# Weight low parts of the second block subtracted on VectorE

## The chip, the cores and the metric

The kernel runs on one core of a Trainium2 chip. The metric is the device time of one execution in microseconds (us). A core has TensorE (PE, matmuls; its weight loads are shown as PEld), VectorE (DVE), ScalarE (ACT), GpSimd (POOL) and SyncE (SP), which here issues the loads of weights. The engines run on their own and meet only at semaphores. Each engine works off its instructions in the order in which they were written, so a wait holds up all that stands behind it on that engine.

## What is computed

Two transformer-like blocks over 512 tokens of width 1024, in float32. The first has a half-step FFN, a mixer of two attentions, and another FFN. The second block, which the change is about, has two layers of this form (cut to what matters):

```python
def hybrid_mixer(h, ...):
    proj = h @ w_in
    qkv, z_a, a_lg, b_lg, cf_val, cf_glu, z_b, gate_lg = split(proj)
    qkv = silu(depthwise_conv_centred(qkv, qkv_conv_w))        # 5 taps, 12 tiles
    q, k, v = split(qkv); q = l2_normalize(q); k = l2_normalize(k)
    o = gated_delta(q, k, v, g_fwd) + flip(gated_delta(flip(q, k, v), g_bwd))
    o = rms(o) * dn_norm_w * silu(z_a)
    u = cf_val * sigmoid(cf_glu)
    u = depthwise_conv_centred(u, cf_conv_w) + cf_conv_b       # 31 taps, 4 tiles
    u = silu(layer_norm(u, cf_ln_w, cf_ln_b)) * silu(z_b)
    gate = sigmoid(gate_lg + gate_b)
    return (gate[0] * (o @ w_dn_out) + gate[1] * (u @ w_cf_out)) @ w_out
```

## The kernel before

**Weights as a stream.** All large weights come as 300 *units* of 128x1024 float32 (512 KB), in the order of use. 132 belong to the two FFNs, 48 to the mixer, 60 to each layer of the second block (the first of them is unit 180). Four slots (`RING`) hold them. Per unit: SyncE loads `raw` once the unit four before is used up; ScalarE casts it to `whi` (a rounded high part, L769); GpSimd subtracts, `wlo = raw - whi` (L1653), in place of `raw`; TensorE then makes three matmuls for each of the eight 128x128 tiles (L303 to L305: high by high, high by low, low by high), in `multiply`. TensorE waits on the semaphore `wlo` before a unit's first matmul. `AHEAD` is 2: cast and subtraction stand in the queues of their engines two units before the unit's use.

**A layer's stages.** `layer` in each engine's function goes through: eight units of value and glu gate (`up`); twelve projection units for q, k and v with the 5-tap convolution on VectorE (L1497 and four times L1500 per tile), the squares and the normalization (`unit_length`, L1485 and L1486); two lead gate units; the delta stage, which is a chunked triangular solve for two directions; eight units for the two `z`; two last gate units; and the merge with eight units of output and eight of the last projection.

**The delta stage** has four chunks (`i`). In each, both directions pass `decay`, `turn`, six levels (a matmul pair, `b.U` on VectorE in L1592, a matmul, `copy_predicated` in L1597; names `level1`, `join1` and so on), then `last`, `keys`, `values`, `out`, and the state update on VectorE (L1603, L1605 or L1607, L1610), on which the next chunk's first matmuls (`d_pre`, L674) wait through `d_snew`. A table, `DELTA_SLOTS`, puts twelve gate units tile by tile into TensorE's time at these named points; ScalarE and GpSimd have a `fill(i, point)` that issues the cast and the subtraction of the unit two ahead where the table starts a unit. Between the answers VectorE works off 56 taps of the 31-tap convolution (`conv(1)`, L1436); the fourth channel's taps are multiplied on ScalarE (L968) and added on GpSimd (L1680).

**The z stage**: VectorE multiplies by `z` (L1541) and splits off low parts (L1544) in a loop of eight.

Of the kernel before, what the change touches and what calls it, by code (L numbers as in the profile page):

```python
# [58 lines left out]
for _name, _n in (("norm", 8), ("qkv_w", 12 * QKV_TAPS), ("cf_w", 4 * CF_TAPS), ("cf_b", 4), ("ln_w", 4),  # L59
# [84 lines left out]
    "wlo xl_even xl_odd unit pair sums scale spread mid ml xr rope rot kc2 vxr vturn blk z1 cmp1 in_mix hidden "  # L144
    "cmp2 kc_raw kc_rot in_w1v kcc vtok vc_raw gate_row cmask expd score probs pt0 pt1 ptc turned o_new pv cw "
    "cturn vcc gts cscore ysum mix_lo h_new yl up wab_lo ab cp ab_raw ab_t sq_qkv ab_read decay sums_qkv l2 gl "
    "cum cum_s filled conv shared mean o_sq o_sums cu_sq var o_dn d_snew d_vns d_pre d_kk d_onew d_qk d_qd "
    "d_at d_a d_t d_u d_ys d_y d_att d_us d_uy d_ttk d_ttv d_kd d_kc d_vt d_kcs d_s0 d_vn d_s d_q d_o in_par "
    "raw0 raw1 raw2 raw3 whi in_h0 in_h1 in_h2 in_h3 square root y xh angle trig sil mh poly tanh gts_sig "
    "negmax csub cexp mix_hi sg yh prod glu_sig qconv qkv root_qkv zero soft_dve soft_act d_eg cum_d d_exp "  # L150
    "z_used cu_c o_root root_cu cu_n cu_silu d_neg d_min d_dec eps dve_step in_pos d_t0 h_out wab_hi out_dma "
# [143 lines left out]
def tensor_engine(pe, m, s):  # L295
# [235 lines left out]
    def merge(g):  # L531
# [4 lines left out]
        for c in range(KD):  # L536
# [3 lines left out]
            pe.wait_ge(s.wlo, u0 + c + 1)  # L540
# [1351 lines left out]
```

## Time and profile before

| | |
|---|---|
| median of three runs | 2611.58 us (2608.43 to 2611.78) |
| the profiled execution | 2605.9 us, of it span 2604.6 us |
| TensorE busy | 2396.9 us (92%) |
| VectorE busy | 1198.7 us (46%) |
| ScalarE busy | 920.5 us (35%) |
| GpSimd busy | 877.7 us (34%), of it L1653 736.9 us |
| chain that ended last | TensorE 76%, VectorE 16%, ScalarE 6%, GpSimd 0% |

Busy time says how long an engine had an instruction running, whether it moved or stood. The chain follows back from the last instruction what released each step. "Idle before" is the time in which an engine had nothing running before an instruction, with the releaser whose signal ended it. The granted clock is the share of full speed that TensorE was given.

### The profile page before, as it was taken

How to read it: one execution, taken by the hardware profiler on the slowest of the kernel's cores; microseconds unless marked ns; L12 is line 12 of the kernel's file. 1: busy time of each engine (PE TensorE's matmuls, PEld its weight loads, DVE VectorE, ACT ScalarE, POOL GpSimd, SP SyncE). 2: the span in 40 equal slices, each digit the busy share in tenths (PEclk: the TensorE clock that was granted, in tenths of full speed). 3: DMA queues.
4: the chain of work that ended last, by engine and by line, in shares of the span. 5: the costliest groups of instructions: out<-in, count | busy, mean ns of one | idle time of the engine just before them, and what ended most of it. 6: DMA issues, size and time to landing. Idle time of an engine off the chain costs nothing.

```text
span 2604.6 us, 29540 instructions
## 1 busy us (share of the span) xinstructions
PE 2396.9 (92%) x12132; PEld 1963.3 (75%) x12132; DVE 1198.7 (46%) x1825; ACT 920.5 (35%) x1532; POOL 877.7 (34%) x428
## 2 busy tenths in 40 slices
PE   5999998989999989999979779999998959999898
PEld 4888786776665868887867568997786748899686
DVE  3000124645655320001247976665536796666632
ACT  3222233233344432222333534444323534433432
POOL 3444443310111444444424522221344433222142
PEclk9999998989999989999979889999998989999998
DMA  3222222200011222222212100000222210000122
GB/s 149 97 98 97 97 97 90 81 25 25 25 33 41 90 69 97 96 96 95 97 41 89 57 25 25 25 25 33 81 98 71 77 47 17 25 26 25 46 96 77
DMA packets 46198, 169.41 MB, mean 65 GB/s; under 512 B 5232, under 2 KB 6000, under 8 KB 45808
## 3 DMA queue, kind: packets, MB, share of 16 engines
q1 hardware_dynamic: 45344, 165.73, 18.6%
q8 instruction: 97, 1.59, 0.2%
q10 hardware_dynamic: 720, 1.79, 0.2%
q14 instruction: 37, 0.30, 0.0%
HBM read 165.40 MB, written 2.10 MB: 64 GB/s over the span
## 4 chain that ended last, share of the span: by engine, by line
PE 76%; DVE 16%; ACT 6%; issue 2%; DMA 0%; POOL 0%; ACTq 0%; DVEq 0%
PE ps L303 18%; PE ps L305 18%; PE ps L304 18%; PE ps L694 4%; PE ps L702 3%; DVE acc L1500 3%; DVE ps L1485 2%; PE ps L691 2%; PE ps L483 2%; PE ps L449 2%; DVE rt L1200 1%; DVE ps L1526 1%; PE ps L464 1%; DVE acc L1497 1%; PE ps L320 1%
## 5 line engine op out<-in xcount | busy, mean ns | idle before, releaser
L1653 POOL TENSOR_TENSOR wlo<-raw,whi 128x1024 fp32r<-128x1024 f32 x300 | 736.9, 2457 | 1331.6 <-ACT whi L769 1331.6
L303 PE MATMUL ps<-xh,whi 128*128 128x512 f32 x1728 | 719.7, 417 | 88.9 <-DVE qkv L1486 28.4
L304 PE MATMUL ps<-xl,whi 128*128 128x512 f32 x1728 | 685.8, 397 | 0.0
L305 PE MATMUL ps<-xh,wlo 128*128 128x512 f32 x1728 | 685.3, 397 | 0.0
L303 PEld LDWEIGHTS ps<-xh,whi 128*128 128x128 f32 x1728 | 332.6, 192 | 197.2 <-issue 50.6
L769 ACT CAST whi<-raw 128x1024 fp32r<-128x1024 f32 x300 | 313.7, 1046 | 271.6 <-DMA raw<-in_stream 196.2
L305 PEld LDWEIGHTS ps<-xh,wlo 128*128 128x128 f32 x1728 | 331.7, 192 | 72.8
L304 PEld LDWEIGHTS ps<-xl,whi 128*128 128x128 f32 x1728 | 333.6, 193 | 64.2 <-issue 4.1
L1236 DVE TENSOR_TENSOR mid<-sil,ps 128x512 f32<-128x512 f32 x44 | 30.3, 688 | 442.8 <-PE ps L305 439.2
L1680 POOL TENSOR_TENSOR cu<-cu,prod 128x512 f32<-128x512 f32 x60 | 83.5, 1391 | 231.1 <-ACT prod L968 231.1
L1436 DVE SCALAR_TENSOR_TENSOR cu<-up,lcols,cu 128x512 f32<-128x512 f32 x180 | 160.0, 909 | 0.7
L303 PE MATMUL ps<-mh,whi 128*128 128x512 f32 x352 | 137.8, 392 | 4.1 <-DVE ml L1239 4.1
L305 PE MATMUL ps<-mh,wlo 128*128 128x512 f32 x352 | 137.6, 391 | 0.0
L304 PE MATMUL ps<-ml,whi 128*128 128x512 f32 x352 | 137.5, 391 | 0.0
L1239 DVE TENSOR_TENSOR ml<-mid,mh 128x512 fp32r<-128x512 f32 x44 | 50.9, 1160 | 175.4 <-ACT mh L812 175.4
L1115 ACT COPY dl<-ps 128x512 f32<-128x512 f32 x96 | 56.3, 586 | 199.7 <-PE ps L694 199.7
L805 ACT ACTIVATE sil<-ps 128x512 f32<-128x512 f32 x44 | 26.3, 598 | 274.7 <-PE ps L305 274.7
L1500 DVE SCALAR_TENSOR_TENSOR acc<-cp,lcols,acc 128x512 f32<-128x512 f32 x96 | 113.6, 1183 | 3.4
L694 PE MATMUL ps<-dl,rt 128*128 128x128 f32 x768 | 107.8, 286 | 0.0
L694 PEld LDWEIGHTS ps<-dl,rt 128*128 128x128 f32 x768 | 99.5, 202 | 0.0
L1597 DVE COPY_PREDICATED dl<-levels,ps 128x512 f32<-128x512 uint8 x96 | 70.5, 738 | 57.4 <-PE ps L702 57.1
L702 PEld LDWEIGHTS ps<-dl 128*128 128x128 f32 x768 | 93.1, 191 | 4.0
(288 smaller groups left out, 3393.6 us busy)
## 6 DMA issues: line engine op xcount, KB each, us to landing
raw<-in_stream SPq DMA_DIRECT2D x300, 512.0 KB, 3.2
w1k<-in_w SPq DMA_DIRECT2D x1, 2048.0 KB, 16.0
w1v<-in_w SPq DMA_DIRECT2D x1, 2048.0 KB, 8.0
outT<-h SPq DMA_DIRECT2D x4, 512.0 KB, 2.7
h<-in_xT ACTq DMA_DIRECT2D x2, 512.0 KB, 6.3
h<-in_xT SPq DMA_DIRECT2D x2, 512.0 KB, 5.9
mats<-in_mats ACTq DMA_DIRECT2D x1, 448.0 KB, 10.3
msk<-in_masks SPq DMA_DIRECT2D x1, 258.0 KB, 12.0
```

Of the source, the lines that this page charges most:

```text
L303: pe.matmul(out, wh, hi, start=first, stop=False)
L304: pe.matmul(out, wh, lo, start=False, stop=False)
L305: return pe.matmul(out, wl, hi, start=False, stop=last)
L694: heads(lambda n, hs: pe.matmul(X[0][:, hs], b.AT[:, n, :], b.T[:, n, :], start=True, stop=True)).then_inc(s.d_y)
L702: heads(lambda n, hs: pe.matmul(X[2][:, hs], b.U[:, n, :], b.Y[:, n, :], start=True, stop=True)).then_inc(s.d_uy)
L769: act.copy(m.whi[:, slot, :], m.raw[:, slot, :]).then_inc(s.whi)
L1115: act.copy(b.Y, X[0]).then_inc(s.d_ys)
L1436: ins = dve.scalar_tensor_tensor(out=dst, in0=src, scalar=w, in1=dst, op0=ALU.mult, op1=ALU.add)
L1500: ins = dve.scalar_tensor_tensor(out=acc, in0=cp[:, k:k + S], scalar=w, in1=acc, op0=ALU.mult, op1=ALU.add)
L1597: dve.copy_predicated(b.T, all_heads(m.levels[:, d, lv, :]), X[2]).then_inc(s.d_t)
L1653: pool.tensor_tensor(m.wlo[:, slot, :], m.raw[:, slot, :], m.whi[:, slot, :].bitcast(F32), ALU.subtract).then_inc(s.wlo)
L1680: pool.tensor_tensor(m.cu[:, 3, :], m.cu[:, 3, :], m.prod[:, k % 2, :], ALU.add).then_inc(s.shared)
```

## The change

The units from the third of the second block on (`POOL_UNITS` = 182 to 299, 118 units) get their low part from VectorE, with a semaphore of its own, `wlo_dve`; GpSimd keeps the first 182. TensorE waits for the one or the other (`low_part`). Everything else stays: the instruction's operands and size, the taps that GpSimd adds, the casts on ScalarE. The core of the diff:

```diff
+POOL_UNITS = 2 * U_FFN + U_MIX + AHEAD
...
+    def low_part(u):
+
+        if u < POOL_UNITS:
+            pe.wait_ge(s.wlo, u + 1)
+        else:
+            pe.wait_ge(s.wlo_dve, u - POOL_UNITS + 1)
...
+    split = POOL_UNITS
+
+    def weights_upto(u):
+
+        nonlocal split
+        while split < min(u, N_UNITS):
+            slot = split % RING
+            dve.wait_ge(s.whi, split + 1)
+            dve.tensor_tensor(m.wlo[:, slot, :], m.raw[:, slot, :], m.whi[:, slot, :].bitcast(F32),
+                              ALU.subtract).then_inc(s.wlo_dve)
+            split += 1
...
         for j in range(12):
             acc, cp = m.acc[:, j % 2, :], m.cp[:, j % 2, :]
+            weights_upto(u0 + L_QKV + j + AHEAD + 1)
             dve.wait_ge(s.cp, 12 * l + j + 1)
...
+        weights_upto(u0 + L_GATE + AHEAD + 1)
         for n in range(4):
             unit_length(4 + n, n)
...
+        weights_upto(u0 + L_GATE + LEAD_UNITS + AHEAD)
         dve.wait_ge(s.d_exp, l + 1)
         delta(l, cf_tap)
+        weights_upto(u0 + L_Z + AHEAD + 2)
...
         for n in range(8):
+            weights_upto(u0 + L_Z + n + AHEAD + 1)
             dve.wait_ge(s.filled, 24 * l + DELTA_UNITS + n + 1)
...
+        def fill(i, point):
+            for n, t0, t1 in DELTA_SLOTS[i, point]:
+                if t0 == 0:
+                    weights_upto(U0_LAYER[l] + L_GATE + n + AHEAD + 1)
...
+                if lv < nl:
+                    fill(i, f"level{lv}")
                 conv(1)
                 if lv < nl:
                     for d, at, X, b, t in both:
                         dve.wait_ge(s.d_uy, level_event(nl - 1, at, lv))
                         dve.copy_predicated(b.T, all_heads(m.levels[:, d, lv, :]), X[2]).then_inc(s.d_t)
+                    fill(i, f"join{lv}")
                     conv(1)
+            for point in ("last", "keys", "values", "out"):
+                fill(i, point)
             for d, at, X, b, t in both:
                 et = m.dsm[:, 3, t, 4 * d:4 * d + 4]
...
-        while split < min(u, N_UNITS):
+        while split < min(u, POOL_UNITS):
```

The same call stands before the tiles of the glu stage, at `decay` and `turn`, and in the merges. In the rows below, the changed kernel's own line numbers stand: L1198 is the new subtraction, and L1461, L1524, L1527, L1633, L1640, L1649, L1651, L1656, L1573 and L1576 are the old L1436, L1497, L1500, L1592, L1597, L1603, L1605, L1610, L1541 and L1544.

First, VectorE in the 5-tap convolution of the first layer. Before, two tiles:

```order
650 L1497 TENSOR_SCALAR acc<-cp,lcols 128x512
651 L1500 SCALAR_TENSOR_TENSOR acc<-cp,lcols,acc 128x512 x4
652 L1497 TENSOR_SCALAR acc<-cp,lcols 128x512
653 L1500 SCALAR_TENSOR_TENSOR acc<-cp,lcols,acc 128x512 x4
654 L1468 TENSOR_SCALAR small<-small 128x32
```

The same two tiles in the changed kernel:

```order
721 L1198 TENSOR_TENSOR wlo<-raw,whi 128x1024 [waits s_whi]
722 L1524 TENSOR_SCALAR acc<-cp,lcols 128x512 [waits s_qkv,s_cp]
723 L1527 SCALAR_TENSOR_TENSOR acc<-cp,lcols,acc 128x512 [waits s_dve_step] x4
724 L1198 TENSOR_TENSOR wlo<-raw,whi 128x1024 [waits s_whi]
725 L1524 TENSOR_SCALAR acc<-cp,lcols 128x512 [waits s_qkv,s_cp]
726 L1527 SCALAR_TENSOR_TENSOR acc<-cp,lcols,acc 128x512 [waits s_dve_step] x4
727 L1494 TENSOR_SCALAR small<-small 128x32 [waits s_soft_act]
```

One subtraction stands before each tile's five instructions.

Second, VectorE in the first chunk of the delta stage, in its third level (changed kernel):

```order
797 L1633 TENSOR_TENSOR dl<-ps,small 128x512 [waits s_d_u] x2
798 L1198 TENSOR_TENSOR wlo<-raw,whi 128x1024 [waits s_whi]
799 L1461 SCALAR_TENSOR_TENSOR cu<-up,lcols,cu 128x512 [waits s_dve_step]
800 L1640 COPY_PREDICATED dl<-levels,ps 128x512 [waits s_d_uy] x2
801 L1461 SCALAR_TENSOR_TENSOR cu<-up,lcols,cu 128x512 [waits s_dve_step]
```

and at that chunk's end, before

```order
727 L1592 TENSOR_TENSOR dl<-ps,small 128x512 x2
728 L1436 SCALAR_TENSOR_TENSOR cu<-up,lcols,cu 128x512
729 L1603 TENSOR_TENSOR rt<-rt,dsm 128x512
730 L1605 COPY o<-ps 128x4x128
731 L1610 TENSOR_TENSOR rt<-rt,ps 128x512
```

and now:

```order
814 L1633 TENSOR_TENSOR dl<-ps,small 128x512 [waits s_d_u] x2
815 L1461 SCALAR_TENSOR_TENSOR cu<-up,lcols,cu 128x512 [waits s_dve_step]
816 L1198 TENSOR_TENSOR wlo<-raw,whi 128x1024 [waits s_whi] x2
817 L1649 TENSOR_TENSOR rt<-rt,dsm 128x512 [waits s_d_o]
818 L1651 COPY o<-ps 128x4x128
819 L1656 TENSOR_TENSOR rt<-rt,ps 128x512 [waits s_dve_step,s_d_s]
```

The subtraction of unit 25 of the layer stands between `b.U` and the tap; those of units 26 and 27 stand between the last tap and the state update.

Third, VectorE in the z stage, in the changed kernel:

```order
905 L1573 TENSOR_TENSOR cu<-cu,prod 128x512
906 L1576 TENSOR_TENSOR fl<-cu,fh 128x512
907 L1573 TENSOR_TENSOR cu<-cu,prod 128x512
908 L1576 TENSOR_TENSOR fl<-cu,fh 128x512
909 L1198 TENSOR_TENSOR wlo<-raw,whi 128x1024
910 L1573 TENSOR_TENSOR cu<-cu,prod 128x512
911 L1576 TENSOR_TENSOR fl<-cu,fh 128x512
```

Row 909 is unit 38 of the layer; on GpSimd nothing stood ahead of it but the subtraction of unit 37.

## Rows read from the trace of the kernel before

**Rows 1.** The page: busy times, and the chain that ended last by engine.

```profile
PE 2396.9 (92%) x12132; PEld 1963.3 (75%) x12132; DVE 1198.7 (46%) x1825; ACT 920.5 (35%) x1532; POOL 877.7 (34%) x428
...
PE 76%; DVE 16%; ACT 6%; issue 2%; DMA 0%; POOL 0%; ACTq 0%; DVEq 0%
```

**Rows 2.** Groups by line and shape: busy us, mean ns, idle before, releaser.

```profile
L1653 POOL TENSOR_TENSOR wlo<-raw,whi 128x1024 fp32r<-128x1024 f32 x300 | 736.9, 2457 | 1331.6 <-ACT whi L769 1331.6
...
L1500 DVE SCALAR_TENSOR_TENSOR acc<-cp,lcols,acc 128x512 f32<-128x512 f32 x96 | 113.6, 1183 | 3.4
...
L1328 DVE TENSOR_REDUCE st<-ps 128x2 f32<-128x1024 f32 x8 | 9.8, 1224 | 0.3
```

**Rows 3.** Timeline of VectorE, convolution and unit_length: start us, us, what, idle.

```profile
1421.61 2.56 DVE L1497 TENSOR_SCALAR acc<-cp,lcols 128x512 f32<-128x512 f32 x1 [4.02 <-ACT cp L1011]
1424.20 6.12 DVE L1500 SCALAR_TENSOR_TENSOR acc<-cp,lcols,acc 128x512 f32<-128x512 f32 x4
...
1437.21 0.48 DVE L1497 TENSOR_SCALAR acc<-cp,lcols 128x512 f32<-128x512 f32 x1
1437.73 3.11 DVE L1500 SCALAR_TENSOR_TENSOR acc<-cp,lcols,acc 128x512 f32<-128x512 f32 x4
...
1486.30 3.36 DVE L1485 RECIPROCAL ps<-ps 128x512 f32<-128x512 f32 x1
...
1508.78 3.37 DVE L1485 RECIPROCAL ps<-ps 128x512 f32<-128x512 f32 x1 [2.86 <-ACT ps L1002]
```

**Rows 4.** Timeline of GpSimd in the same stretch.

```profile
1424.88 1.29 POOL L1680 TENSOR_TENSOR cu<-cu,prod 128x512 f32<-128x512 f32 x1 [1.00 <-ACT prod L968]
1426.13 2.86 POOL L1653 TENSOR_TENSOR wlo<-raw,whi 128x1024 fp32r<-128x1024 f32 x1
```

**Rows 5.** Stretches: length, busy us of PE, PEld, DVE, ACT, POOL; PEclk, DMA.

```profile
1480.00:1486.00 6.00, 0.00 (x0) 0.00 (x0) 5.86 (x5) 2.14 (x4) 4.34 (x3) 0.50 0.00 0
...
1836.00:1842.00 6.00, 5.34 (x17) 4.29 (x18) 4.48 (x5) 4.15 (x7) 2.88 (x2) 0.72 0.00 0
```

**Rows 6.** Timeline of all engines, first chunk of the delta stage, third level.

```profile
1556.34 0.74 DVE L1436 SCALAR_TENSOR_TENSOR cu<-up,lcols,cu 128x512 f32<-128x512 f32 x1
...
1557.10 1.05 ACT L769 CAST whi<-raw 128x1024 fp32r<-128x1024 f32 x1
...
1558.05 0.72 ACT L968 ACTIVATE prod<-up,lcols 128x512 f32<-128x512 f32 x1
1558.20 0.74 DVE L1597 COPY_PREDICATED dl<-levels,ps 128x512 f32<-128x512 uint8 x1 [1.12 <-PE ps L702]
...
1559.59 0.60 PE L691 MATMUL ps<-mats,dl 128*128 128x128 f32 x4
...
1567.38 0.69 DVE L1592 TENSOR_TENSOR dl<-ps,small 128x512 f32<-128x512 f32 x1 [0.49 <-PE ps L691]
```

**Rows 7.** Timelines of VectorE, TensorE and ScalarE at the first three chunk boundaries.

```profile
1592.91 0.69 DVE L1603 TENSOR_TENSOR rt<-rt,dsm 128x512 f32<-128x512 f32 x1 [12.11 <-PE ps L736]
...
1597.47 1.05 PE L674 MATMUL ps<-mats,small 128*128 128x128 f32 x8
...
1597.56 1.03 ACT L769 CAST whi<-raw 128x1024 fp32r<-128x1024 f32 x1
...
1664.06 1.04 ACT L769 CAST whi<-raw 128x1024 fp32r<-128x1024 f32 x1
...
1665.76 1.13 DVE L1566 TENSOR_SCALAR dl<-ps,dsm 128x128 f32<-128x128 f32 x4 [1.09 <-PE ps L674]
...
1728.11 1.92 DVE L1603 TENSOR_TENSOR rt<-rt,dsm 128x512 f32<-128x512 f32 x1 [11.96 <-PE ps L736]
```

**Rows 8.** Timelines of TensorE, ScalarE and VectorE in the z stage.

```profile
1836.66 0.50 PE L303 MATMUL ps<-xh,whi 128*128 128x512 f32 x1 [3.67 <-ACT prod L1052]
...
1808.41 1.03 ACT L769 CAST whi<-raw 128x1024 fp32r<-128x1024 f32 x1
...
1838.12 0.69 DVE L1544 TENSOR_TENSOR fl<-cu,fh 128x512 fp32r<-128x512 f32 x1 [0.69 <-ACT fh L1073]
```

More of the change, by code:

```diff
@@ L143 @@
 SIGNALS = (
[L144 to L151, printed above, removed]
+    "wlo wlo_dve xl_even xl_odd unit pair sums scale spread mid ml xr rope rot kc2 vxr vturn blk z1 cmp1 "
+    "in_mix hidden cmp2 kc_raw kc_rot in_w1v kcc vtok vc_raw gate_row cmask expd score probs pt0 pt1 ptc "
+    "turned o_new pv cw cturn vcc gts cscore ysum mix_lo h_new yl up wab_lo ab cp ab_raw ab_t sq_qkv ab_read "
+    "decay sums_qkv l2 gl cum cum_s filled conv shared mean o_sq o_sums cu_sq var o_dn d_snew d_vns d_pre d_kk "
+    "d_onew d_qk d_qd d_at d_a d_t d_u d_ys d_y d_att d_us d_uy d_ttk d_ttv d_kd d_kc d_vt d_kcs d_s0 d_vn d_s "
+    "d_q d_o in_par raw0 raw1 raw2 raw3 whi in_h0 in_h1 in_h2 in_h3 square root y xh angle trig sil mh poly "
+    "tanh gts_sig negmax csub cexp mix_hi sg yh prod glu_sig qconv qkv root_qkv zero soft_dve soft_act d_eg "
+    "cum_d d_exp z_used cu_c o_root root_cu cu_n cu_silu d_neg d_min d_dec eps dve_step in_pos d_t0 h_out "
+    "wab_hi out_dma "
 )
@@ L305, in multiply @@
         return pe.matmul(out, wl, hi, start=False, stop=last)
+    def low_part(u):
[3 more added lines that the diff above has]
+            pe.wait_ge(s.wlo_dve, u - POOL_UNITS + 1)
     def x_unit(u, out, x_ready=None):
-        pe.wait_ge(s.wlo, u + 1)
+        low_part(u)
         for k in range(KD):
@@ L346, in ffn @@
             u = u0 + 2 * NF + i
-            pe.wait_ge(s.wlo, u + 1)
+            low_part(u)
             pe.wait_ge(s.ml, NF * f + i + 1)
@@ L434, in gates @@
                         pe.wait_ge(s.cmask, 4 * call + 4)
-                    pe.wait_ge(s.wlo, u0 + n + 1)
+                    low_part(u0 + n)
                 for t in range(t0, t1):
@@ L539, in merge @@
                 pe.wait_ge(s.ysum, 8 * g + c - 1)
-            pe.wait_ge(s.wlo, u0 + c + 1)
+            low_part(u0 + c)
             for r in (0, 1) if mixer else (1, 0):
@@ L551, in merge @@
         for c in range(KD):
-            pe.wait_ge(s.wlo, u0 + c + 1)
+            low_part(u0 + c)
             if c >= 4:
@@ L643, in gate_tiles @@
         if t0 == 0:
-            pe.wait_ge(s.wlo, u + 1)
+            low_part(u)
             if n >= 2:
@@ L1405, in merge @@
             p, bank = c % 2, 2 * (c % 2)
+            if not mixer:
+                weights_upto(u0 + c + AHEAD + 1)
             if mixer:
@@ L1420, in merge @@
         for c in range(KD):
+            if not mixer:
+                weights_upto(u0 + c + AHEAD + 1)
             dve.wait_ge(s.unit, u0 + c + 1)
@@ L1442, in layer @@
         for c in range(4):
+            weights_upto(u0 + 2 * c + AHEAD + 2)
             dve.wait_ge(s.glu_sig, 4 * l + c + 1)
@@ L1528, in layer @@
                                      op0=ALU.mult, op1=ALU.mult).then_inc(s.o_dn)
+        weights_upto(u0 + L_Z + AHEAD + 2)
         dve.wait_ge(s.root_cu, l + 1)
@@ L1544, in layer @@
             dve.tensor_tensor(m.fl[:, k, :], dst, m.fh[:, k, :].bitcast(F32), ALU.subtract).then_inc(s.mix_lo)
+        weights_upto(u0 + L_OUT + AHEAD)
     def delta(l, cf_tap):
@@ L1580, in delta @@
                 be = m.small[:, 9, t, 4 * d:4 * d + 4]
+                if d == 0:
+                    fill(i, "decay")
+                    fill(i, "turn")
                 dve.wait_ge(s.d_a, at + 1)
```

## The prediction

> **What bounds the kernel now.** The page's busy times and the chain that ended last come first [rows 1]: TensorE is busy 92% of the span and holds 76% of the chain, VectorE 16%, GpSimd nothing. So GpSimd's time, 737 us of it weight subtractions of 2457 ns each [rows 2], is not itself a cost. What matters is the second block, where the 16% of VectorE lies. There I read VectorE's timeline beside GpSimd's.
>
> In the projection and short convolution (units 8 to 19 of a layer), VectorE sets the pace. A convolution of one tile is a `tensor_scalar` of 0.48 us and four chained multiply-adds of 3.11 us when nothing disturbs them, but 2.56 and 6.12 us when GpSimd runs beside them [rows 3]. GpSimd's tap and subtraction at 1424.88 and 1426.13 lie exactly over the stretched multiply-adds [rows 4]. From 1421.61 to 1486.30 nine convolutions take 64.7 us.
>
> In the delta stage TensorE is the bound and VectorE answers it: in each level VectorE idles 1.12 + 0.49 us [rows 6]. Whatever is put between VectorE's answers has only that room.
>
> **What the change does, by place.** 118 of the 300 subtractions go to VectorE. Its price there is not in the trace; one VectorE pass over 128x1024 float32 is 1224 ns in the reduction [rows 2], so I take 1.22 us, and 1.2 to 2.5 as bounds (the upper end is GpSimd's own figure). The rest of the change is where VectorE's queue now stops to wait for the `whi` cast of ScalarE. All terms are for one layer; the second layer's trace repeats the first 625.5 us later.
>
> (a) Convolution, a gain. A convolution becomes 0.5 + 3.1 + 1.2 (subtraction) + 1.0 (GpSimd's tap of 1.29 us still blocks one multiply-add) = 5.8 us. Nine of them are 52.4, with ten small softplus instructions of about 0.2 us in all 54.4 instead of 64.7: **-10.3 us**. Bounds: -14 (the taps also fall into gaps) to -3 (the subtraction costs 2 us). TensorE has run out of work by the last of the nine (nothing in 1480 to 1486, [rows 5]), so it takes little of the gain away. GpSimd's instructions over the gated units before this (glu stage) hide under TensorE both ways.
>
> (b) The subtraction before the twelfth convolution lies between `unit_length` calls, where nothing was blocked before: **+1.2**. The next one fits in the 2.86 us for which VectorE waits for the roots at 1508.78 [rows 3]: 0. The one before `delta` waits for a cast that ScalarE issues only after the exponentials, about 3 us; but the second direction's `d_pre` came that late already, and GpSimd no longer blocks the mask product: 0.
>
> (c) Chunk boundaries. After each chunk's levels VectorE now takes the subtractions of `last`, `keys`, `values` and `out` ahead of the state update (L1603 to L1610). The cast for `out` stands in ScalarE's queue behind the sigmoid of a gate unit that TensorE finishes in that same fill. At the first boundary the cast ends at 1597.56 + 1.04 = 1598.6; VectorE subtracts until 1599.8, and the three instructions of the update (0.6 each) set `d_snew` at 1601.7. TensorE asks for it at 1597.47 [rows 7]: **+4.3**. At the second the cast ends at 1665.1, the state is new at 1668.2, and TensorE was ready 1.1 us before the 1665.76 row, at 1664.7: **+3.6**. At the third the update starts at 1728.11 and takes 1.92 instead of 0.69, blocked by GpSimd's subtraction: the cast was done before TensorE was, and the subtraction moves into that wait: 0. At the fourth there is none. These waits are certain by order; what could soften them is only where a wait ends.
>
> (d) Inside levels, before the tap (units 25, 31, 32). For unit 25 VectorE is free at 1557.1, the cast runs until 1558.15, the subtraction until 1559.4. GpSimd's tap, whose product is ready at 1558.8, then takes its 1.3 us, the tap on VectorE 0.7: the `copy_predicated` that started at 1558.20 starts at about 1561.3, 3.1 late. It ended 0.65 before TensorE used it at 1559.59 [rows 6]: **+2.4**. Unit 31 has the same neighbours: **+2.4**. Unit 32 lies in level 6, without a GpSimd tap and with more slack: 0 to 1.2, taken **+0.4**. Bounds of the three together: 1.5 (no tap in between) to 7.
>
> These same two places rest on the rows that show VectorE standing still for a whole GpSimd instruction, and not slowed in proportion [rows 3, 4]. The Trainium skill, "SBUF — State Buffer", section "Who interferes with whom", says it as a rule: an instruction with two SBUF inputs on VectorE contends with a GpSimd instruction that reads SBUF, the pair is held for the whole instruction, and the earlier one has it. By that rule the level terms stand as above; were the port shared in halves, they would be some 1.3 us less each.
>
> (e) At joins (units 28, 29, 34, 35) the subtraction stands after the copies; the 1.6 us of idle time of a level [rows 6] covers 1.22 unless the cast is late or a tap comes between. I take 0.45 each, **+1.8**, bounds 0 to 5.
>
> (f) After the delta stage the loop over `z` asks for unit 38 one step late: TensorE wants it at 1836.66; the cast of 1808.41 was ready long before, but VectorE has it in its queue behind the second `fl` (1838.12 + 0.69), so it ends at 1840.0 [rows 8]: **+3.4**. From there to the layer's end (units 39 to 61) each subtraction is done a unit or more ahead of TensorE, which is the bound there: 0.
>
> (g) TensorE's clock. After the idle 3.67 us before 1836.66, the granted clock of the next 6 us was 0.72 of full speed, that is half speed (1.2 GHz) for part of it [rows 5]: 0.28 x 6 = 1.7 us of work lost. The two boundaries of (c) leave TensorE idle as long where it was busy before: 2 x 1.7 = **+3.4**, bounds 0 to 7 (four such places).
>
> Sum for a layer: -10.3 + 1.2 + 7.9 + 5.2 + 1.8 + 3.4 + 3.4 = +12.6; two layers +25.2 us. The profiled execution (span 2604.6 us, 2605.9 with what lies around it) becomes 2631. The median shown is 2611.6, 5.7 above it, so I predict **2637**.
>
> **The rivals.**
> 1. The contention weighs more and the waits less: *faster*. The mechanism is (a) alone: VectorE is blocked for some 26 us in the nine convolutions of a layer, and without the subtractions the stage falls to TensorE's own pace. If (c) to (g) were all hidden, 2611.6 - 2 x 9.1 = 2593. It decides from the point where their sum is under 9 us a layer. For it speaks that VectorE is on the chain there; against it that boundary and `z` waits alone, read from order and end times, are 11.3. Chance 0.08.
> 2. They cancel: no clock loss, no tap in between, joins free, and the convolution at its better bound -14: -14 + 1.2 + 7.9 + 1.5 + 3.4 = 0, so 2612. Chance 0.08.
> 3. VectorE becomes the bound of the convolution as before: its new subtraction is blocked by the taps and costs 2 us, so that (a) gives 3 instead of 10.3. Then 2637 + 14.6 = 2652; with slow clocks at all four places 2659. For it speaks that VectorE is full in that stage; against it that the same instruction of GpSimd blocked for 2 us and is gone. Chance 0.2.
> 4. The change does not do what it says: GpSimd keeps the work. The order of instructions excludes it: 118 rows stand on VectorE, none on GpSimd. 0.
>
> **How the numbers follow.** The forecast has 0.64. Its own range is 2622 to 2650, from the bounds of (a), (d) and (g). To hold 8 in 10, I reach down to the cancelling case and up over rival 3: 2611 to 2656. Within 0.2% (about what a measurement of this kernel tells from no change, 5 us either way) lie rival 2 and a little of the forecast's low edge: 0.09. Faster: 0.08. Slower: 0.83.
>
> **What would show it.** Right if: the multiply-adds of the convolution fall from 1183 ns to about 950 ns; the nine convolutions take about 54 us; L1603's counterpart waits for the cast at the first two boundaries and TensorE then idles 4 us before the `d_pre` matmuls; `ps` of unit 38 waits 3.4 us for VectorE; idle time of VectorE's subtraction is put down to ScalarE's `whi`. Wrong if the chunk period (67 us before) does not grow by 6 to 10 us in the first chunk, if VectorE's subtraction takes far from 1.22 us, or if TensorE's waits for VectorE in the delta stage stay under 10 us a layer.

## The result and the profile after

The changed kernel takes **2630.36 us** (median of 4 runs, 2626.26 to 2631.99), the kernel before, on the same chip, 2610.01 us (2606.55 to 2611.78). The ratio is 1.0077, with a 95% interval of 1.006 to 1.0095: slower by 20.4 us. Forecast was slower by 25.4 us, 2637 with 2611 to 2656 as the range. The direction, the waits and their places came out as forecast; the gain in the convolutions and the places of the clock drops did not quite.

The page of the changed kernel: busy times, VectorE's and GpSimd's low parts, and the chain by engine. It answers to [rows 1] and [rows 2].

```profile
PE 2404.7 (92%) x12132; PEld 1969.5 (75%) x12132; DVE 1253.5 (48%) x1943; ACT 921.0 (35%) x1532; POOL 582.5 (22%) x310
...
PE 74%; DVE 17%; ACT 6%; issue 2%; DMA 0%; POOL 0%; ACTq 0%; DVEq 0%
...
L1699 POOL TENSOR_TENSOR wlo<-raw,whi 128x1024 fp32r<-128x1024 f32 x182 | 441.2, 2424 | 797.0 <-ACT whi L778 797.0
L1198 DVE TENSOR_TENSOR wlo<-raw,whi 128x1024 fp32r<-128x1024 f32 x118 | 145.5, 1238 | 148.5 <-ACT whi L778 148.4
```

GpSimd lost 295 us of work and the kernel became slower. The 118 subtractions cost VectorE 1238 ns each (the guess from the reduction was 1.22 us), and ahead of them VectorE stood still for 148.4 us, waiting for the cast `whi` of ScalarE. That wait is new: before, GpSimd waited for the same casts, and behind them in its queue stood only its own taps; GpSimd is not on the chain that ended last [rows 1, 2].

VectorE in the changed kernel's convolution (start us, us, what, idle before), and below it GpSimd's two taps in that stretch. They answer to [rows 3] and [rows 4].

```profile
1422.59 0.47 DVE L1524 TENSOR_SCALAR acc<-cp,lcols 128x512 f32<-128x512 f32 x1
...
1446.08 4.01 DVE L1527 SCALAR_TENSOR_TENSOR acc<-cp,lcols,acc 128x512 f32<-128x512 f32 x4
1450.02 1.21 DVE L1198 TENSOR_TENSOR wlo<-raw,whi 128x1024 fp32r<-128x1024 f32 x1
1451.15 0.47 DVE L1524 TENSOR_SCALAR acc<-cp,lcols 128x512 f32<-128x512 f32 x1
1451.66 4.02 DVE L1527 SCALAR_TENSOR_TENSOR acc<-cp,lcols,acc 128x512 f32<-128x512 f32 x4
...
1463.80 1.51 DVE L1524 TENSOR_SCALAR acc<-cp,lcols 128x512 f32<-128x512 f32 x1
1465.35 3.12 DVE L1527 SCALAR_TENSOR_TENSOR acc<-cp,lcols,acc 128x512 f32<-128x512 f32 x4
...
1473.94 3.36 DVE L1511 RECIPROCAL ps<-ps 128x512 f32<-128x512 f32 x1
```

```profile
1448.00 1.54 POOL L1726 TENSOR_TENSOR cu<-cu,prod 128x512 f32<-128x512 f32 x1 [5.69 <-ACT prod L977]
...
1463.55 1.48 POOL L1726 TENSOR_TENSOR cu<-cu,prod 128x512 f32<-128x512 f32 x1 [4.27 <-ACT prod L977]
```

Four multiply-adds take 4.01 us with one tap of GpSimd beside them and 3.12 without, as in term (a). The stage that ended at 1486.30 [rows 3] now ends at 1473.94.

The first chunk boundary of the changed kernel, ScalarE, VectorE and TensorE. It answers to [rows 7].

```profile
1588.69 0.69 ACT L984 ACTIVATE sg<-ps,lcols 128x512 f32<-128x512 f32 x1 [7.55 <-PE ps L307]
1589.27 1.03 ACT L778 CAST whi<-raw 128x1024 fp32r<-128x1024 f32 x1
...
1590.34 1.23 DVE L1198 TENSOR_TENSOR wlo<-raw,whi 128x1024 fp32r<-128x1024 f32 x1 [13.38 <-ACT whi L778]
1591.48 0.68 DVE L1649 TENSOR_TENSOR rt<-rt,dsm 128x512 f32<-128x512 f32 x1
...
1592.68 0.68 DVE L1656 TENSOR_TENSOR rt<-rt,ps 128x512 f32<-128x512 f32 x1
...
1593.42 2.08 PE L683 MATMUL ps<-mats,small 128*128 128x128 f32 x8 [4.08 <-DVE rt L1656]
```

This is the chain of term (c) step by step: the sigmoid of the gate unit, behind it the cast, behind it the subtraction, then the update (L1649 to L1656), then TensorE, which stood for 4.08 us. At the second boundary the row reads 3.38. Before, TensorE did not stand at either.

### The profile page after: what moved, and what is told of

Read it like the earlier page. It is cut to its first block, busy times and chain, and to the rows that moved or that the text cites. A ratio compares the mean times of both kernels' runs of the same rounds, so it can differ in the third digit from the quotient of the medians.

```text
span 2625.0 us, 29544 instructions
## 1 busy us (share of the span) xinstructions
PE 2404.7 (92%) x12132; PEld 1969.5 (75%) x12132; DVE 1253.5 (48%) x1943; ACT 921.0 (35%) x1532; POOL 582.5 (22%) x310
## 4 chain that ended last, share of the span: by engine, by line
PE 74%; DVE 17%; ACT 6%; issue 2%; DMA 0%; POOL 0%; ACTq 0%; DVEq 0%
PE ps L305 18%; PE ps L307 18%; PE ps L306 18%; PE ps L703 3%; PE ps L711 3%; DVE acc L1527 3%; DVE ps L1511 2%; PE ps L492 2%; PE ps L700 2%; DVE wlo L1198 2%; PE ps L458 2%; DVE rt L1221 1%; DVE ps L1556 1%; PE ps L473 1%; PE ps L329 1%
## 5 line engine op out<-in xcount | busy, mean ns | idle before, releaser
L1699 POOL TENSOR_TENSOR wlo<-raw,whi 128x1024 fp32r<-128x1024 f32 x182 | 441.2, 2424 | 797.0 <-ACT whi L778 797.0
L1198 DVE TENSOR_TENSOR wlo<-raw,whi 128x1024 fp32r<-128x1024 f32 x118 | 145.5, 1238 | 148.5 <-ACT whi L778 148.4
L1461 DVE SCALAR_TENSOR_TENSOR cu<-up,lcols,cu 128x512 f32<-128x512 f32 x180 | 137.1, 782 | 0.7
L711 PEld LDWEIGHTS ps<-dl 128*128 128x128 f32 x768 | 92.8, 191 | 7.4 <-DVE dl L1633 3.6
L711 PE MATMUL ps<-dl 128*128 128x128 f32 x768 | 93.8, 275 | 1.9 <-DVE dl L1633 1.9
## 6 DMA issues: line engine op xcount, KB each, us to landing
mats<-in_mats ACTq DMA_DIRECT2D x1, 448.0 KB, 10.4
```

The costliest lines, as they stand in the source:

```text
L711: heads(lambda n, hs: pe.matmul(X[2][:, hs], b.U[:, n, :], b.Y[:, n, :], start=True, stop=True)).then_inc(s.d_uy)
L1198: dve.tensor_tensor(m.wlo[:, slot, :], m.raw[:, slot, :], m.whi[:, slot, :].bitcast(F32), ALU.subtract).then_inc(s.wlo_dve)
L1461: ins = dve.scalar_tensor_tensor(out=dst, in0=src, scalar=w, in1=dst, op0=ALU.mult, op1=ALU.add)
L1699: pool.tensor_tensor(m.wlo[:, slot, :], m.raw[:, slot, :], m.whi[:, slot, :].bitcast(F32), ALU.subtract).then_inc(s.wlo)
```

## Where the time went, by stage

The profiled executions differ by up to 6 us before the second block begins, where all kernels here do the same work (in ten of the eleven experiments that follow, the first `up` product of layer 1 came 4.5 to 5.8 us later than in the trace of the kernel before, in the changed kernel and in e3 it came 0.04 to 0.06 earlier). So stages are compared from marker to marker. The markers are instructions of VectorE in each trace: the first `up` product, the first reciprocal of `unit_length`, the first of the second direction's four mask instructions (before: L1566) of each chunk, the last L1603, the last addition to `h`. Each entry is what a stage gained or lost against the kernel before, in us, the mean of both layers; the names of the experiments are explained below.

| | up to unit_length | to chunk 1 | chunk 1 | chunk 2 | chunk 3 | chunk 4 | z to end | a layer |
|---|---|---|---|---|---|---|---|---|
| forecast | -10.3 | +1.2 | +8.4 | +6.2 | +2.8 | +0.9 | +3.4 | +12.6 |
| changed kernel | -12.3 | +1.6 | +9.6 | +4.5 | +2.2 | +0.5 | +4.1 | +10.2 |
| e1 conv units | -10.4 | +0.1 | +0.1 | 0.0 | 0.0 | 0.0 | 0.0 | -10.1 |
| e2 other units | -1.9 | +1.6 | +9.5 | +4.5 | +2.3 | +0.6 | +4.1 | +20.6 |
| e3 out behind update | -12.3 | +1.6 | +3.3 | +1.7 | +0.8 | +0.5 | +4.3 | -0.1 |
| e4 z earlier | -12.3 | +1.7 | +8.9 | +4.5 | +2.3 | +0.5 | +1.3 | +6.9 |
| e5 levels late | -12.3 | +1.6 | +5.4 | +5.8 | -1.8 | +0.5 | +5.0 | +4.2 |
| e6 three moves | -12.3 | +1.6 | +0.1 | +1.6 | -1.5 | +0.5 | +2.4 | -7.5 |
| e7 small taps | -14.7 | +1.4 | +10.2 | +4.5 | +2.2 | +0.6 | +4.2 | +8.4 |
| e8 subtract twice | -0.3 | +1.4 | +9.8 | +4.5 | +2.2 | +0.6 | +4.1 | +22.3 |
| e9 fitted | -12.3 | +0.5 | -0.1 | +1.7 | -0.6 | +2.8 | +0.8 | -7.2 |
| e10 z in gap | -12.3 | +1.4 | +9.7 | +4.4 | +2.2 | +0.5 | +0.4 | +6.5 |
| e11 four moves | -12.3 | +0.3 | +0.6 | +1.7 | -1.5 | +0.5 | +0.3 | -10.5 |

The forecast's row sorts its terms by the same marks: chunk 1 holds unit 25, the first boundary and one clock drop; chunk 2 two joins, the second boundary and the other drop; chunk 3 units 31 and 32; chunk 4 two joins. Two layers of +10.2 are the 20.4 us of the runs. The two layers of the changed kernel agree within 0.1 us but for the first two chunks, which took +9.1 and +5.2 in layer 1 and +10.0 and +3.7 in layer 2.

## The experiments

### Gain and costs apart

One function decides who subtracts a unit; `r` counts units within a layer. For e1:

```diff
+def on_vector(u):
+    if u < POOL_UNITS:
+        return False
+    r = (u - POOL_UNITS + AHEAD) % U_LAYER
+    return 10 <= r < 21
```

> Only the eleven subtractions that VectorE takes in the convolution loop (units 10 to 20 of a layer) stay on VectorE; GpSimd keeps all others, at their old places. Theory (the change is one gain in the convolutions and several waits behind it): the gain alone is left. The delta stage of layer 1 started 11.2 us earlier in the changed kernel and 12.4 us at the first unit_length; I expect 11 to 12.4 us a layer, 2610 - 23 = 2587 us. Rival A (the gain is given back behind the stage, because TensorE has to do the same work anyway): 2605 to 2610. Rival B (the gain in the stage also needs VectorE's other subtractions): 2600.

Measured: **2589.84 us** against 2610.28, ratio 0.992 (0.9907 to 0.9933). The theory holds, with 10.2 us a layer where 11 to 12.4 were expected (unit 21 makes the difference, see e2). The table says it more sharply: -10.4 us until `unit_length`, and then next to nothing in any stage up to the layer's end, so the gain is kept whole.

For e2 the last line is `return not 10 <= r < 21`.

> The complement: units 10 to 20 of each layer on GpSimd as before, all others of the second block on VectorE. Theory: the costs alone, 10.2 us a layer net in the changed kernel plus the 11 to 12.4 of the gain, so +43 to +46 us: 2653 to 2656. Rival A (gain and costs are not independent, because a delta stage that starts earlier runs into casts and weights that come no earlier): 2630 to 2640. Rival B (there was no real gain, the waits alone are the +20): 2630.

Measured: **2652.83 us**, ratio 1.0171 (1.0157 to 1.0184). Gain and costs add up: -10.1 and +20.6 a layer make +10.5 where the whole change has +10.2, and the stages add up one by one. The -1.9 in the first stage, which e1 lacks, comes from one of the other units: 21, whose subtraction GpSimd made during the eleventh convolution, the last before `unit_length`. The multiply-adds of that convolution before the change, GpSimd beside them, and the same multiply-adds in e2, where GpSimd has only its tap there:

```profile
1480.42 5.96 DVE L1500 SCALAR_TENSOR_TENSOR acc<-cp,lcols,acc 128x512 f32<-128x512 f32 x4
...
1482.25 2.79 POOL L1653 TENSOR_TENSOR wlo<-raw,whi 128x1024 fp32r<-128x1024 f32 x1
```

```profile
1486.28 4.00 DVE L1533 SCALAR_TENSOR_TENSOR acc<-cp,lcols,acc 128x512 f32<-128x512 f32 x4
```

Up to the start of that convolution e2 is within 0.1 us of the kernel before.

### The chunk boundaries

```diff
-            for point in ("last", "keys", "values", "out"):
+            for point in ("last", "keys", "values"):
                 fill(i, point)
...
                 dve.tensor_tensor(b.St, b.St, X[0], ALU.add).then_inc(s.d_snew)
+            fill(i, "out")
```

> The changed kernel, but VectorE takes the subtraction of the point out behind the state update and not ahead of it. Theory (term c of the prediction): TensorE idles 4.08 and 3.38 us at the first two boundaries for that update, and its next matmuls then run at half speed and lose 2.4 and 1.8 us. Both go; the subtraction, now between the update and the mask product, gives back up to 1.2 us at each of three boundaries. 9 to 11 us a layer: 2630.4 - 20 = 2610 (2607 to 2613). Rival (TensorE's wait there is set by the state update itself and not by the subtraction): 0 to -5, 2626 to 2630.

Measured: **2610.19 us**, ratio 0.9999 (0.999 to 1.0008). Moving the subtraction of `out` alone takes off as much as the changed kernel lost: 20.2 us are gone, with 118 subtractions still on VectorE. TensorE's waits of 4.08 and 3.38 us are not there any more. But term (c) and its two clock drops are not all of it: in chunk 3, to which they add nothing, e3 is 1.4 us faster than the changed kernel, and what it lacks there is a third clock drop (see the clock, below). VectorE at the same boundary of e3:

```profile
1584.53 0.69 DVE L1649 TENSOR_TENSOR rt<-rt,dsm 128x512 f32<-128x512 f32 x1 [7.65 <-PE ps L745]
...
1590.23 1.23 DVE L1198 TENSOR_TENSOR wlo<-raw,whi 128x1024 fp32r<-128x1024 f32 x1 [1.14 <-ACT whi L778]
1591.38 1.12 DVE L1604 TENSOR_SCALAR dl<-ps,dsm 128x128 f32<-128x128 f32 x4
```

The update starts as soon as TensorE's matmul (L745) lets it, 5.7 us before the subtraction, where in the changed kernel it stood 1.1 us behind it. The subtraction now sits directly ahead of the mask instruction L1604, and what that costs is in the table's +3.3, +1.7 and +0.8 of the first three chunks, beside the level and join terms, which e3 leaves.

### Inside the levels

```diff
-                if lv < nl:
-                    fill(i, f"level{lv}")
                 conv(1)
...
                         dve.copy_predicated(b.T, all_heads(m.levels[:, d, lv, :]), X[2]).then_inc(s.d_t)
+                    fill(i, f"level{lv}")
```

> The changed kernel, but VectorE takes the subtractions of the level points (units 25, 31, 32) behind the two copy_predicated of that level and not ahead of the convolution tap. Theory (term d): TensorE's waits of 2.02 us for copy_predicated at units 25 and 31 and 0.57 at unit 32 go, and the subtraction at its new place costs 0 to 0.5 each, as at the joins: 4 to 4.6 us a layer off, 2630.4 - 9 = 2621.5. Rival (it is the tap on VectorE, blocked by GpSimd's tap, that makes the copies late, wherever the subtraction stands): 0, 2630.

Measured: **2617.69 us**, ratio 1.0029 (1.002 to 1.0038), 12.7 us less than the changed kernel, where 9 was expected. VectorE of the changed kernel at unit 25, and TensorE behind it:

```profile
1547.62 1.23 DVE L1198 TENSOR_TENSOR wlo<-raw,whi 128x1024 fp32r<-128x1024 f32 x1 [1.76 <-ACT whi L778]
1548.76 1.76 DVE L1461 SCALAR_TENSOR_TENSOR cu<-up,lcols,cu 128x512 f32<-128x512 f32 x1
1550.44 1.33 DVE L1640 COPY_PREDICATED dl<-levels,ps 128x512 f32<-128x512 uint8 x2
...
1551.21 0.66 PE L700 MATMUL ps<-mats,dl 128*128 128x128 f32 x4 [2.02 <-DVE dl L1640]
```

These are term (d)'s three parts: the wait for the cast, the subtraction, and the tap that GpSimd's tap holds up (1.76 instead of 0.74 us). e5 at the same level:

```profile
1552.98 0.75 DVE L1638 COPY_PREDICATED dl<-levels,ps 128x512 f32<-128x512 uint8 x1 [0.15 <-PE ps L711]
1553.61 1.49 DVE L1198 TENSOR_TENSOR wlo<-raw,whi 128x1024 fp32r<-128x1024 f32 x1
1555.03 0.74 DVE L1461 SCALAR_TENSOR_TENSOR cu<-up,lcols,cu 128x512 f32<-128x512 f32 x1
```

With the same subtraction behind the copies, TensorE's waits of 2.02 us at units 25 and 31 and of 0.57 us at unit 32 are gone, 4.6 us a layer. The clock drop behind unit 31, 1.7 us (below), went with them; together they make 6.3 us a layer, which is what the runs show. The match is in part luck: the stages sum to 5.9, and other drops changed too (in e5 the 6 us from 1668 have a granted clock of 0.50; chunk 1 gained 4.2 us and not 2.0, chunk 2 and z lost 1.3 and 0.9). In chunk 3, e5 is 1.8 us *faster* than the kernel before the change, because that one has a clock drop there too and e5 has none.

### The z stage

e4 takes unit 38 ahead of the last reciprocal:

```diff
-        weights_upto(u0 + L_Z + AHEAD + 2)
+        weights_upto(u0 + L_Z + AHEAD + 3)
         dve.wait_ge(s.root_cu, l + 1)
```

> The changed kernel, but unit 38 is subtracted before the last reciprocal and the cu products, ahead of the loop over z. Theory (term f): TensorE's wait before that unit falls from 7.1 us to the 3.67 us that ScalarE's prod caused before: -3.4 us a layer, 2630.4 - 7 = 2623.5. Rival (the wait is ScalarE's anyway, or the subtraction at its new place delays the cu products and with them the silu and the later z units): 0, 2630.

Measured: **2625.49 us**, ratio 1.0059 (1.0047 to 1.0071), 4.9 less than the changed kernel, where 7 was expected. The theory had the wait right, and the expectation overlooked what its rival names: at the new place the subtraction stands on VectorE's chain to the `cu` products. TensorE ahead of unit 38 in the changed kernel, then VectorE and TensorE in e4:

```profile
1846.77 0.77 PE L305 MATMUL ps<-xh,whi 128*128 128x512 f32 x1 [7.11 <-DVE wlo L1198]
```

```profile
1840.59 1.22 DVE L1198 TENSOR_TENSOR wlo<-raw,whi 128x1024 fp32r<-128x1024 f32 x1
1841.72 3.36 DVE L1561 RECIPROCAL ps<-ps 128x512 f32<-128x512 f32 x1
...
1849.82 0.80 PE L305 MATMUL ps<-xh,whi 128*128 128x512 f32 x1 [4.78 <-ACT prod L1061]
```

The wait for VectorE's `wlo` is gone, but the one for ScalarE's `prod` that is left is 4.78 us long and not 3.67 as before the change [rows 8]: 1.1 us, one subtraction, came back. So e10 puts the subtraction where VectorE waits 4.5 us for the first root:

```diff
                                      op0=ALU.mult, op1=ALU.add).then_inc(s.cu_c)
+        weights_upto(u0 + L_Z + AHEAD + 3)
         for c in range(4):
             dve.wait_ge(s.o_root, 4 * l + c + 1)
```

> The changed kernel with one edit: unit 38 is subtracted in VectorE's 4.5 us wait for the first root, and not (as in the run before) between the last o product and the reciprocal, where it stood 1.2 us long ahead of the cu products. Theory: from the last state update to the layer's end the changed kernel loses 4.1 us against the one before, the run with the earlier subtraction 1.3; in the gap it loses 0 to 0.4. So 3.7 to 4.1 us a layer, 2630.4 - 7.8 = 2622.6. Rival (the place does not matter once the subtraction is ahead of the loop): 2625.5, as there.

Measured: **2622.16 us**, ratio 1.0042 (1.0029 to 1.0056). TensorE's wait is 3.60 us again, and from the last update to the layer's end 0.4 us remain of 4.1, as expected.

### What sets the convolution stage

In e7 GpSimd's taps of this stage are short: the kernel leaves out 496 of their 512 columns, so its output is not the right one and only its time is of use; in e8 each of the eleven subtractions is made twice:

```diff
-            pool.tensor_tensor(m.cu[:, 3, :], m.cu[:, 3, :], m.prod[:, k % 2, :], ALU.add).then_inc(s.shared)
+            n = 16 if k < POOL_TAPS_QKV else S
+            pool.tensor_tensor(m.cu[:, 3, 0:n], m.cu[:, 3, 0:n], m.prod[:, k % 2, 0:n], ALU.add).then_inc(s.shared)
```

```diff
             dve.wait_ge(s.whi, split + 1)
+            if 10 <= (split - POOL_UNITS + AHEAD) % U_LAYER < 21:
+                then(dve.tensor_tensor(m.sg[:, 0:2, :].rearrange("p a b -> p (a b)"), m.raw[:, slot, :],
+                                       m.whi[:, slot, :].bitcast(F32), ALU.subtract))
```

> The changed kernel with work left out: GpSimd's eleven taps of the convolution stage add only 16 of 512 columns, so that they are short. Theory (VectorE is blocked by a tap for 0.9 us per convolution, and TensorE's unit of 5.6 us is the floor under VectorE's 5.7): the four multiply-adds take 3.12 us everywhere, but a step of the stage only falls to 5.6, so 1 to 4 us a layer, 2623 to 2628. Rival A (VectorE alone sets the stage, and TensorE could follow): 9 times 0.9 = 8 us a layer, 2614. Rival B (the 4.0 us of the multiply-adds have nothing to do with GpSimd): no change, 2630.

> The changed kernel with one more subtraction of the same size and inputs (into a tile that is not in use) ahead of each of the eleven in the convolution loop. It prices VectorE's subtraction in place, and with the run of the short taps tells which engine sets the stage. Theory (VectorE has no idle time there, so it sets the stage, with TensorE just under it): 1.15 to 1.2 us each, 11 times, 12.5 to 13.5 us a layer, 2655 to 2658. Rival A (TensorE sets the stage and VectorE has slack): under 5 us a layer, below 2640. Rival B (a second pass collides with more of GpSimd's taps and costs 2 us): 2670 or more.

Measured: e7 **2627.29 us**, ratio 1.0058 (1.0045 to 1.0071); e8 **2655.23 us**, ratio 1.0169 (1.0155 to 1.0183). The groups of VectorE's multiply-adds in the changed kernel and in e7, and VectorE's timeline in e7:

```profile
L1527 DVE SCALAR_TENSOR_TENSOR acc<-cp,lcols,acc 128x512 f32<-128x512 f32 x96 | 86.9, 905 | 3.4
```

```profile
L1527 DVE SCALAR_TENSOR_TENSOR acc<-cp,lcols,acc 128x512 f32<-128x512 f32 x96 | 72.2, 752 | 3.4
```

```profile
1445.44 1.23 DVE L1198 TENSOR_TENSOR wlo<-raw,whi 128x1024 fp32r<-128x1024 f32 x1 [0.30 <-ACT whi L778]
1447.61 0.49 DVE L1524 TENSOR_SCALAR acc<-cp,lcols 128x512 f32<-128x512 f32 x1 [0.95 <-ACT cp L1020]
1448.14 3.11 DVE L1527 SCALAR_TENSOR_TENSOR acc<-cp,lcols,acc 128x512 f32<-128x512 f32 x4
```

With short taps the multiply-adds are 752 ns throughout, so what stretches them (1183 before [rows 2], 905 after) is GpSimd's instructions. But the stage gains only 2.4 us a layer (-14.7 instead of -12.3): VectorE now idles for `cp`, the copy of TensorE's product, and the chain of work from 1421 to 1471 lies to 88% on TensorE, where in the changed kernel (1421 to 1474) it lies to over 80% on VectorE. A second subtraction, in turn, costs 12.0 us a layer for eleven, 1.1 each, so nothing of it is hidden. VectorE sets the stage, and TensorE lies close under it (in the changed kernel it is busy for the whole of 1410 to 1470, before for 56.5 of these 60 us): there is nearly nothing more to gain here.

One rival the forecast does not name. In this stage of the kernel before, TensorE stood three times for GpSimd's `wlo`, 4.1 us in all, once like this:

```profile
1444.45 0.47 PE L303 MATMUL ps<-xh,whi 128*128 128x512 f32 x1 [1.15 <-POOL wlo L1653]
```

So a slow GpSimd could have been the cause by itself, without blocking VectorE. The chain of work from 1421 to 1490 speaks against it: 67% of it are VectorE's convolutions (L1497, L1500), and GpSimd is not on it; its casts came late because ScalarE stood behind VectorE's `acc`, as in the 3.33 us before its instruction at 1437.01.

### All subtractions on VectorE, without the waits

e6 joins the edits of e3, e4 and e5.

> The changed kernel with three edits: out behind the state update, unit 38 ahead of the last reciprocal, level subtractions behind the copies. Theory (the costs are separate waits and add up): 2630.4 - 20.2 - 4.9 - 9 = 2596, within 3. Rival A (removing one wait makes room that the next fills, so the edits overlap): 2601 to 2607. Rival B (without GpSimd's subtractions the delta stage becomes faster than it was before the change, since the chunk starts gained 0.9 to 1.7 us): 2586 to 2592, better than the kernel with VectorE's subtractions in the convolutions alone (2589.8).

Measured: **2596.67 us**, ratio 0.9947 (0.9934 to 0.9959), within the expected range. That range had been set with 9 us for e5; with its measured 12.7 the three savings sum to 37.7 us, and together they give 33.7. So the costs add up but for 4 us. The drop of the clock in chunk 3, which e3 and e5 each lose and e6 can lose only once, is 3.4 us in two layers, near that. All 118 subtractions on VectorE are faster than the kernel before by 13.7 us, once none of them stands ahead of an answer that TensorE needs.

e9 has the edits of e5 and e10, and two more: unit 21 moves into the wait for the roots, and `out` of a chunk behind the mask instructions of the next.

```diff
-            weights_upto(u0 + L_QKV + j + AHEAD + 1)
+            weights_upto(u0 + L_QKV + min(j, 10) + AHEAD + 1)
...
                 ins.then_inc(s.d_min)
+            if i:
+                fill(i - 1, "out")
             conv(1)
```

> All 118 subtractions on VectorE as in the changed kernel, each put where the traces show VectorE idle: level points behind the copies, out behind the two mask instructions of the next chunk (where VectorE waits for the exponential), unit 38 in the 4.5 us wait for the first root, unit 21 in the wait for the roots of the unit lengths. Theory (every cost of the change was a wait of its own, so what the run with three moves still loses against the gain in the convolutions are three subtractions of 1.2 us that stand on VectorE's path: ahead of the cu products, between update and mask, between the unit lengths): 2596.7 - 2 x (1.2 + 1.5 + 1.2) = 2589, within 3. Rival A (the delta stage has no room for them at all, and the remaining loss stays): 2594 to 2597. Rival B (the delta stage without GpSimd's subtractions is faster than before): 2583 to 2586, faster than the split with the convolution units alone.

Measured: **2596.79 us**, ratio 0.9944 (0.9931 to 0.9958). The expected 2589 was wrong, and rival A has the number; but not its reason, as the table shows: against e6 the z stage gained (+0.8 for +2.4), unit 21 gained (+0.5 for +1.6), and the new place of `out` lost it, above all in chunk 4 (+2.8 for +0.5: +3.9 in layer 1 and +1.7 in layer 2). VectorE in e9 at the third chunk's start, TensorE at the fourth's, and the stretch behind it (length, busy us of PE, PEld, DVE, ACT, POOL; PEclk):

```profile
1665.43 1.13 DVE L1605 TENSOR_SCALAR dl<-ps,dsm 128x128 f32<-128x128 f32 x4 [1.55 <-PE ps L683]
1666.48 1.22 DVE L1198 TENSOR_TENSOR wlo<-raw,whi 128x1024 fp32r<-128x1024 f32 x1
1667.61 0.75 DVE L1461 SCALAR_TENSOR_TENSOR cu<-up,lcols,cu 128x512 f32<-128x512 f32 x1
1668.27 1.28 DVE L1613 SCALAR_TENSOR_TENSOR rt<-ps,dl 128x512 f32<-128x512 f32 x2
```

```profile
1741.08 1.11 PE L700 MATMUL ps<-mats,dl 128*128 128x128 f32 x4 [2.66 <-DVE dl L1631]
```

```profile
1740.00:1750.00 10.00, 8.92 (x48) 8.52 (x49) 5.55 (x9) 4.06 (x6) 0.23 (x1) 0.66 0.14 48
```

I had taken the wait for the exponential for a gap. The tap L1461 already filled it, and subtraction and tap together put off L1613, which begins the chain to TensorE. TensorE idled 2.66 us at L700 (1.73 in e6), and in the 10 us from 1740 it had a mean of 0.66 of full speed. In layer 2 no such drop followed, which is the difference between +3.9 and +1.7. e11 is e9 with `out` back directly behind the update, as in e3.

> As the run with all subtractions fitted, but out again directly behind the state update, as in the run with three moves. Theory (what the fitted run lost is the subtraction on the way to the chunk's first mask product: TensorE idled 2.66 us at each chunk start instead of 1.7 to 1.9, and at the fourth it then ran at 0.66 clock for 10 us; the other two new places gained): the fitted run's chunk 4 loss of 3.9 us goes and the z gain stays: 2592, within 2. Rival A (out costs the same there, on the way to the mask as well): 2596.5. Rival B (with all places right it falls under the kernel with the convolution units alone): 2587 or less.

Measured: **2591.04 us**, ratio 0.9927 (0.9914 to 0.9939). Chunk 4 is back at +0.5 and the z gain stays, as expected. So the loss was the place of `out`. e11, with everything on VectorE, and e1, with eleven units a layer, have overlapping intervals; both beat both kernels by 19 to 41 us. e1 needs no search for gaps.

## Why the prediction was right, and where it was off

**(a) The convolutions: too small.** -10.3 forecast, -12.3 measured. The nine convolutions took 51.4 us (1422.59 to 1473.94) where 54.4 were forecast. A step takes 5.58 us (1446.08 to 1451.66) and not 5.8; and between these marks lie eight subtractions, not nine, since the first stands ahead of its mark. One us of this is given back ahead of the marks: before, VectorE waited 4.02 us for `cp` there [rows 3], now 3.54 us for a cast and then 1.5 us of subtraction. That GpSimd's instructions over the glu stage hide both ways was right: the first convolution starts 44.2 us behind the first `up` product before the change, after it and in e2. The price of the subtraction was right (1.22 from a reduction of the same size; 1238 ns in the mean, 1.1 us on the path in e8), so rival 3, with 2 us, is out.

**(b) +1.2 up to chunk 1:** measured +1.6; in e9 and e11, with the subtraction of unit 21 moved into the wait for the roots, +0.5 and +0.3. The one before `delta` does wait for its cast, 3.14 us, and the first direction's mask comes 4.5 us later, counted from the first reciprocal; the second direction's was late already, as forecast, and loses only the 1.6.

**(c) Boundaries, +4.3 and +3.6:** TensorE stood for 4.08 and 3.38 us, and e3, with the subtraction behind the update, has neither. What was read from the order and from end times alone held.

**(d) Levels, +2.4 each for units 25 and 31, +0.4 for 32:** TensorE idled 2.02, 2.02 and 0.57 us, 4.6 against the 5.2 forecast, and e5 shows that they were these. What (d) and (g) had at nothing is the clock drop behind unit 31. **(e) Joins:** two waits of 0.47 us in front of L711, at units 28 and 34, two of nothing; forecast 0.45 for each of four, so 0.9 us a layer for 1.8.

**(f) z, +3.4:** TensorE's idle time grew from 3.67 [rows 8] to 7.11 us, by 3.44. The stage lost 4.1, and e10 gets 3.7 back.

**(g) The clock, +3.4: near as a sum, wrong in part by place.** Stretches of the kernel before, then of the changed one, then of e3:

```profile
1676.00:1686.00 10.00, 10.00 (x71) 9.70 (x70) 6.39 (x11) 4.35 (x6) 1.27 (x1) 0.83 0.16 50
```

```profile
1593.00:1599.00 6.00, 5.58 (x29) 5.58 (x30) 3.28 (x8) 1.11 (x2) 1.11 (x1) 0.57 0.00 1
...
1666.00:1671.00 5.00, 4.53 (x26) 4.53 (x27) 3.33 (x8) 1.11 (x2) 0.06 (x1) 0.66 0.00 0
...
1677.00:1687.00 10.00, 8.28 (x66) 7.57 (x65) 7.85 (x12) 4.19 (x6) 1.27 (x1) 1.00 0.07 20
...
1693.00:1699.00 6.00, 5.94 (x36) 5.82 (x37) 3.20 (x6) 1.79 (x3) 0.11 (x1) 0.72 0.01 1
```

```profile
1684.00:1690.00 6.00, 6.00 (x49) 5.70 (x50) 4.49 (x8) 1.79 (x3) 1.28 (x1) 1.00 0.00 1
```

Behind the two waits of (c) the granted clock is 0.57 and 0.66, so 0.43 x 6 = 2.6 and 0.34 x 5 = 1.7 us are lost (0.2 of the 2.6 while TensorE still stood), 4.1 for the forecast's 3.4. Two things the forecast did not look for come on top. There is a third new drop, behind the 2.02 us wait of unit 31: 0.28 x 6 = 1.7 us. And the kernel before had drops of its own: in layer 1 the one above at the third chunk's start (0.17 x 10 = 1.7 us), where the changed kernel has full speed, in layer 2 one each in chunks 2 and 3 (0.72 over the 6 us from 2236 and from 2304). So in chunk 3 of layer 1 an old drop went and a new one came, and they cancel. For the whole program, TensorE's busy time grew from 2396.9 to 2404.7 us, 3.9 a layer, with the same 12132 instructions; e3 has 2396.6 again. The last row is e3's stretch behind unit 31, where TensorE waits 2.02 us as well: full speed, so the wait alone does not bring the drop.

So the misses are: (a) by 2.0 us too small a gain; (b) forecast 0.4, chunk 1 1.2 and z 0.7 too low, against chunks 2, 3 and 4 forecast 1.7, 0.6 and 0.4 too high. The misses of the costs nearly cancel: all costs together were forecast as +22.9 a layer and are +22.5. That they come so close is in part luck; each wait was read within 0.5 us of what the trace then showed, but the clock was placed wrong.

**Of the signs named,** the multiply-adds fell to 905 ns (950 said), the nine convolutions took 51.4 us (54 said), L1649 waits behind the cast, unit 38 waits 3.4 us longer, the idle time ahead of the subtraction is put down to `whi`, and the first chunk grew by 9.1 and 10.0 us in the two layers (6 to 10 said). The new waits for VectorE in the delta stage of layer 1 are 13.0 us (2.02, 4.08, 0.47, 3.38, 2.02, 0.57 and 0.47), so rivals 1 and 2 are out; e1, though, is rival 1's kernel: its 2593 was computed for (a) without the waits, and 2590 was measured.

**The rule on the port.** In the rows above, a tap of GpSimd that began at 1463.55 makes the `tensor_scalar` of 1463.80 last 1.51 instead of 0.48 us; the added 1.03 us take it to 1465.3, just beyond the tap's end at 1465.0. It stood still and was not slowed in proportion. The Trainium skill, "SBUF — State Buffer", section "Who interferes with whom", says of the SBUF ports that the two engines share that the instruction that issues first has them for its whole length, and that the other is fully blocked. These rows agree with it, and so does the level row at 1548.76 (1.76 instead of 0.74 us).

## What to carry to other kernels

Work that is moved from an idle engine to one with half its time free is paid for by its place in the queue: on VectorE a subtraction of 1.2 us cost 0 where VectorE waited anyway, 1.2 where it did not, and up to 6.5 (4.08 + 2.4) where it had to wait for a cast in front of an answer that TensorE needed, the clock drop behind the wait included. So list, for every moved instruction, what stands behind it and when its input is ready; put it behind the answer, not ahead of it. And before using a gap, look at what is already in it (e9), and whether the instruction behind it is on the chain (e4).

## What the hardware did that was not expected

- The clock after a wait is not told by the wait's length alone. In layer 1 of e9 TensorE idled 2.66 us at the start of chunks 3 and 4; the 10 us from 1674 had full clock, the 10 us from 1740 had 0.66. In the kernel before, 1.93 us at the third chunk was followed by 0.83. The wait of 2.02 us at unit 31 was followed by 0.72 in the changed kernel and by full clock in e3. What decides between them was not found.
- An instruction that reads one large tile, and not two, is blocked by GpSimd too: `tensor_scalar` 0.48 us alone, 1.51 beside a tap.
- Executions of one kernel spread over 6 us (the kernel before: 2605.77 to 2612.11), and the traces, one of each kernel, put such differences into the first block, where all kernels here are alike. So the profiled execution of the kernel before, 2605.9, is one of its shortest, and differences of stages had to be taken from markers within the second block.
